# Spreading inverse roots by float32r products over twin rows in a two-block transformer kernel

## What is computed

```python
def first_block(x, mem, ...):
    for layer in range(DEPTH):
        h = rms_norm(x, mix_norm_g[layer])
        proj = h @ w_in[layer]
        da_q, da_k, da_v, sb_q, sb_k, sb_v, c_q, c_kv, k_r = jnp.split(proj, pts, axis=-1)
        y_a = diff_attention(da_q, da_k, ...)      # q and k normed per head of 64
        y_b = stick_breaking(sb_q, sb_k, sb_v, ...)
        y_c = latent_attention(c_q, c_kv, k_r, ...) # q and k normed per head of 96: 64 plain, 32 rotary
        y = jnp.concatenate([y_a, y_b, y_c], axis=-1)
        x = x + y @ w_out[layer]
        ...
```

## Time and profile before

| | us |
|---|---|
| median of 3 runs | 2628.76 (2628.24 to 2629.06) |
| profiled execution | 2626.96 |
| span in that execution, first to last instruction | 2625.2 |
| TensorE busy | 2572.9, 98% |
| GpSimd busy | 1313.6, 50% |
| VectorE busy | 1142.8, 44% |
| ScalarE busy | 677.7, 26% |
| mean granted clock of TensorE | 0.998 |

### The profile page before, as it was taken

One profiled execution on the slowest core, in us unless ns is written; L12 is line 12 of the kernel. 1 busy time (PEld: TensorE's weight loads), 2 busy tenths in 40 slices (PEclk: granted clock), 3 DMA queues, 4 the chain that ended last, 5 costly groups with the idle time before them and its releaser, 6 DMA issues.

```text
span 2625.2 us, 35579 instructions
## 1 busy us (share of the span) xinstructions
PE 2572.9 (98%) x14733; PEld 2058.6 (78%) x14733; DVE 1142.8 (44%) x1977; ACT 677.7 (26%) x1329; POOL 1313.6 (50%) x548
## 2 busy tenths in 40 slices
PE   7999999999999999999999999999999999999998
PEld 6877668888888776688888866888888877888887
DVE  4344464666543445546665345322224135322224
ACT  4236451111122454511111244200001333200002
POOL 5443136665565432255555732566555521566653
PEclk9999999999999999999999999999999999999999
DMA  7321124555332110335663211322222211222221
GB/s 246 95 59 33 33 90 135 193 189 185 120 100 81 59 48 29 102 118 188 191 192 113 84 49 33 107 96 96 96 96 96 81 49 33 81 96 96 96 96 64
DMA packets 222509, 265.38 MB, mean 101 GB/s; under 512 B 19248, under 2 KB 197000, under 8 KB 222248
## 3 DMA queue, kind: packets, MB, share of 16 engines
q1 hardware_dynamic: 219648, 256.58, 30.7%
q10 hardware_dynamic: 2728, 6.90, 0.8%
HBM read 258.74 MB, written 4.72 MB: 100 GB/s over the span
## 4 chain that ended last, share of the span: by engine, by line
PE 69%; ACT 1%; DVE 1%; POOL 0%; issue 0%; PEldq 0%; PEld 0%; DVEq 0%; ACTq 0%
PE PS L961 8%; PE PS L964 8%; PE PS L965 8%; PE PS L923 4%; PE PS L927 4%; PE PS L928 4%; PE PS L1672 2%; PE PS L1676 2%; PE PS L1675 2%; PE PS L1958 1%; PE PS L2011 1%; PE PS L1832 1%; PE PS L1799 1%; PE PS L942 1%; PE PS L945 1%; PE PS L948 1%
## 5 line engine op out<-in xcount | busy, mean ns | idle before, releaser
L833 POOL TENSOR_SCALAR WH<-RAW 128x2048 fp32r<-128x2048 f32 x178 | 342.2, 1923 | 1099.1 <-issue 906.5
L835 POOL TENSOR_TENSOR WL<-RAW,WH 128x2048 fp32r<-128x2048 f32 x178 | 822.5, 4621 | 14.8
L961 PE MATMUL PS<-Hh,WL 128*128 128x512 f32 x1152 | 448.6, 389 | 0.0
L964 PE MATMUL PS<-Hl,WH 128*128 128x512 f32 x1152 | 448.2, 389 | 0.0
L965 PE MATMUL PS<-Hh,WH 128*128 128x512 f32 x1152 | 448.1, 389 | 0.0
L2625 DVE SCALAR_TENSOR_TENSOR X<-PS,X 128x512 f32<-128x512 f32 x304 | 208.8, 689 | 189.4 <-PE PS L1676 127.6
L961 PEld LDWEIGHTS PS<-Hh,WL 128*128 128x128 f32 x1152 | 216.3, 188 | 45.3 <-issue 0.4
L965 PEld LDWEIGHTS PS<-Hh,WH 128*128 128x128 f32 x1152 | 216.3, 188 | 45.0
L964 PEld LDWEIGHTS PS<-Hl,WH 128*128 128x128 f32 x1152 | 216.3, 188 | 44.5
L3005 DVE TENSOR_TENSOR PS<-SQ,PS 128x512 f32<-128x512 f32 x44 | 30.6, 696 | 427.6 <-PE PS L965 427.6
L1672 PE MATMUL PS<-U,WL 128*128 128x512 f32 x512 | 202.3, 395 | 0.0
(11 more groups left out here) (550 smaller groups left out, 4703.9 us busy)
## 6 DMA issues: line engine op xcount, KB each, us to landing
RAW<-in_w_ff SPq DMA_DIRECT2D x64, 1024.0 KB, 5.5
PROJ<-in_ada_w SPq DMA_DIRECT2D x48, 1024.0 KB, 8.2
RAW<-in_ffn_w_in SPq DMA_DIRECT2D x44, 1024.0 KB, 5.1
RAW<-in_ffn_w_out SPq DMA_DIRECT2D x22, 1024.0 KB, 4.8
RAW<-in_w_in SPq DMA_DIRECT2D x20, 1024.0 KB, 5.5
RAW<-in_w_out SPq DMA_DIRECT2D x8, 1024.0 KB, 5.0
RAW<-in_a_w_in SPq DMA_DIRECT2D x6, 1024.0 KB, 5.1
RAW<-in_b_w_in SPq DMA_DIRECT2D x12, 512.0 KB, 4.6
```

Of the source, the lines that this page charges most:

```text
L833: pool.tensor_scalar(WH[b][:, :], RAW[b][:, :], 1.0, 1.0, ALU.mult, ALU.mult).then_inc(s.split_hi, 1)
L835: pool.tensor_tensor(WL[b][:, :], RAW[b][:, :], WH[b][:, :].bitcast(F32), ALU.subtract).then_inc(s.split_done, 1)
L961: ins = mm(bank, WL[b][:, col:col + P], Hh[:, k, :], start=k == 0, stop=False)
L964: mm(bank, WH[b][:, col:col + P], Hl[:, k, :], start=False, stop=False)
```

## The change

The spreads are made by single float32r products over tiles that hold twin rows. In each group of 32 rows, rows 0 to 15 hold the high half and rows 16 to 31 the rest of the same values; a spread matrix with ones in both rows adds them in one product.

- The column patterns that sum squares get their ones twice, 16 columns apart, so sums, roots and inverses come out in both rows.
- Head norms: VectorE's subtract (2663) becomes one scalar_tensor_tensor, which takes off the high half in the second of the twin rows only. `head_spread` makes four products instead of eight.
- Latents: ScalarE leaves the root in PS. VectorE inverts it there, copies it to float32r (`roots_hi`), and fills the twins by four scalar_tensor_tensor of 32 rows by 128 columns into a tile of 128x512 that it has set to zero at the start of the stage. TensorE makes six products over 512 columns (`latents_spread`) in the place of six calls of `token_spread`.
- The spread matrices grow from 2 to 6, so their transfer (line 715) from 128 to 384 KB and VectorE's turn to float32r from 256 to 768 columns.
- Two masks leave the constants and come by a transfer of their own (128 KB, 256 columns), issued ahead of the memory's; a third, unused one is dropped. VectorE waits for it with its first copy.
- A semaphore is saved in the memory attention, where `me.r` becomes a count of `me.m`.
- The list of the output steps and all else stays in its order.

```diff
@@ position_constants
-    c[0:HD, C_HALF] = 1
-    c[HD:P, C_HALF + 1] = 1
+    for twin in (0, TWIN):
+        c[0:HD, C_HALF + twin] = 1
+        c[HD:P, C_HALF + twin + 1] = 1
...
-    spread = np.zeros((P, 2, P), np.float32)
-    for b in range(2):
-        spread[2 * b:P:32, b, 0:HD] = 1
-        spread[2 * b + 1:P:32, b, HD:P] = 1
+    spread = np.zeros((P, SPREADS, P), np.float32)
+    for b in range(4):
+        spread[2 * b:P:TWIN, b, 0:HD] = 1
+        spread[2 * b + 1:P:TWIN, b, HD:P] = 1
+    for x in range(2):
+        for h in range(MLA_HEADS):
+            spread[4 * x + h:P:TWIN, 4 + x, MLA_ROPE * h:MLA_ROPE * h + MLA_ROPE] = 1
@@ transfers
+            sp.dma_start(masks_in, t["dist"][:, D_ALL:D_ALL + 2 * P]).then_inc(s.hot_in, 16)
...
-            sp.dma_start(PTS[:, 1, 0:256].rearrange("p (b c) -> p b c", b=2), t["spread"]).then_inc(s.lam_in, 16)
+            sp.dma_start(spread_in.rearrange("p (b c) -> p b c", b=SPREADS), t["spread"]).then_inc(s.lam_in, 16)
@@ head_spread
-                    mm(PS[:, banks[g], 0:n], spread[32 * g:32 * g + 32, q, :], inv_h[32 * g:32 * g + 32, 0:n], start=True, stop=False)
-                for g in range(4):
-                    n = width(4 * q + g)
-                    mm(PS[:, banks[g], 0:n], spread[32 * g:32 * g + 32, q, :], inv_l[32 * g:32 * g + 32, 0:n],
-                       start=False, stop=True).then_inc(a.bc, 1)
+                    mm(PS[:, banks[g], 0:n], spread[32 * g:32 * g + 32, q, :], inv_twins[32 * g:32 * g + 32, 0:n],
+                       start=True, stop=True).then_inc(a.bc, 1)
@@ TensorE, second stage
+                def latents_spread(bank, kind):
+
+                    mm(bank, spread[:, kind, :], twins, start=True, stop=True).then_inc(s.f_tile, 1)
+
...
                 for x in range(4):
-                    token_spread(feed(11 + x), TN_ML, 2 * x)
+                    latents_spread(feed(11 + x), x)
                 for x in range(2):
-                    token_spread(feed(15 + x), TN_ML, 4 * x, MLA_ROPE)
+                    latents_spread(feed(15 + x), 4 + x)
@@ ScalarE
-                    f(roots(n), PS[:, bank, 0:P], ACT.Sqrt, scale=scale, bias=bias).then_inc(mix.rt, 1)
+                    f(PS[:, bank, 0:P] if n == TN_ML else roots(n), PS[:, bank, 0:P], ACT.Sqrt, scale=scale, bias=bias).then_inc(mix.rt, 1)
@@ VectorE
-                v.tensor_tensor(inv_l, PS[:, 7, :], inv_h.bitcast(F32), ALU.subtract).then_inc(s.hri, 1)
+                v.scalar_tensor_tensor(inv_twins, inv_h.bitcast(F32), twin, PS[:, 7, :], ALU.mult, ALU.add).then_inc(s.hri, 1)
...
-            v.wait_ge(s.hot_in, 32)
+            v.wait_ge(s.hot_in, 48)
...
-            v.tensor_copy(spread[:, :, :], PTS[:, 1, 0:256].rearrange("p (b c) -> p b c", b=2))
+            v.tensor_copy(spread[:, :, :], spread_in.rearrange("p (b c) -> p b c", b=SPREADS))
...
+                def latents_inverse():
+
+                    root = PS[:, 5, 0:P]
+                    v.wait_ge(mix.rt, tn + TN_ML + 1)
+                    v.reciprocal(root, root).then_inc(mix.r_ml, 1)
+                    v.wait_ge(mix.r_ml, 2 * L + 1)
+                    v.tensor_copy(roots_hi, root).then_inc(mix.r_ml, 1)
+                    v.wait_ge(mix.r_ml, 2 * L + 2)
+                    for c in range(QT):
+                        r = slice(32 * c, 32 * c + 32)
+                        ins = v.scalar_tensor_tensor(twins[r, P * c:P * c + P], roots_hi[r, :].bitcast(F32), twin[r, :], root[r, :],
+                                                     ALU.mult, ALU.add)
+                    ins.then_inc(mix.r, 1)
+
+                v.memset(twins.bitcast(F32), 0.0)
...
-                token_inverse(TN_ML)
+                latents_inverse()
```

More of the change, by code:

```diff
@@ L89 @@
 SLOTS = 3
-C_ID, C_ONE, C_NTRI, C_NONE, C_SBM, C_SBN, C_RECT = [P * i for i in range(7)]
-C_EPS = C_RECT + P
+C_ID, C_ONE, C_NTRI, C_NONE = [P * i for i in range(4)]
+C_EPS = C_NONE + P
 C_SLA = C_EPS + 1
@@ L103 @@
 C_SEL = C_MX + 32
-C_ALL = C_SEL + 12 + 32
+C_TWIN = C_SEL + 12 + 32
+C_ALL = C_TWIN + 1
+TWIN = 16
+SPREADS = 6
 DIL_KEYS = S + 2 * P
@@ L131, in position_constants @@
     c[:, C_NONE:C_NONE + P] = -1
-    c[:, C_SBM:C_SBM + P] = p < f
-    c[:, C_SBN:C_SBN + P] = np.where(p < f, 0, NEG)
-    c[:, C_RECT:C_RECT + P] = np.where(f // CHUNK > p // CHUNK, NEG, 0)
     half = MLA_ROPE // 2
@@ L144, in position_constants @@
         c[:, C_SLB + o] = HD ** -0.5 / dil_slope(2 * o + np.arange(P) // HD)
-    c[0:HD, C_HALF] = 1
-    c[HD:P, C_HALF + 1] = 1
+    for twin in (0, TWIN):
+        c[0:HD, C_HALF + twin] = 1
+        c[HD:P, C_HALF + twin + 1] = 1
     c[:, C_WHOLE:C_WHOLE + 2] = 0.5
     for h in range(MLA_HEADS):
-        c[MLA_ROPE * h:MLA_ROPE * h + MLA_ROPE, C_QUART + h] = 1
-    c[:, C_CQ:C_CQ + MLA_HEADS] = MLA_DIM * EPS / 256
+        c[MLA_ROPE * h:MLA_ROPE * h + MLA_ROPE, [C_QUART + h, C_QUART + TWIN + h]] = 1
+    for twin in (0, TWIN):
+        c[:, C_CQ + twin:C_CQ + twin + MLA_HEADS] = MLA_DIM * EPS / 256
     c[:, C_MX:C_MX + MEM_HEADS] = HD * EPS / D
     c[:, C_SEL + 12] = 1
-    c[:, C_MLB] = np.where(np.arange(P) % 32 < MLA_HEADS, EPS * EPS, EPS)
+    c[:, C_MLB] = np.where(np.arange(P) % TWIN < MLA_HEADS, EPS * EPS, EPS)
+    c[:, C_TWIN] = -(np.arange(P) % 32 >= TWIN).astype(np.float32)
     c[:, C_YCB] = np.where(np.arange(P) % 32 < 2, 0, EPS)
-    spread = np.zeros((P, 2, P), np.float32)
-    for b in range(2):
-        spread[2 * b:P:32, b, 0:HD] = 1
-        spread[2 * b + 1:P:32, b, HD:P] = 1
+    spread = np.zeros((P, SPREADS, P), np.float32)
[5 more added lines that the diff above has]
+            spread[4 * x + h:P:TWIN, 4 + x, MLA_ROPE * h:MLA_ROPE * h + MLA_ROPE] = 1
     freqs = (np.float32(10000.0) ** (-np.arange(half, dtype=np.float32) / np.float32(half))).astype(np.float32)
@@ L177, in position_constants @@
     far = 1e30
-    d = np.zeros((P, D_ALL), np.float32)
+    d = np.zeros((P, D_ALL + 2 * P), np.float32)
+    d[:, D_ALL:D_ALL + P] = np.where(p < f, 0, NEG)
+    d[:, D_ALL + P:] = np.where(f // CHUNK > p // CHUNK, NEG, 0)
     u = np.arange(3 * P)[None, :]
@@ L288, in __init__ @@
         self.r = sem("mx_r")
+        self.r_ml = sem("mx_r_ml")
         self.yn = sem("mx_yn")
@@ L343, in __init__ @@
         self.tr = sem("me_tr")
-        self.r = sem("me_r")
         self.s = sem("me_s")
@@ L419, in build @@
         PROJR = nc.alloc_sbuf_tensor_at("PROJR", [P, 18, S], F32R, offset=proj_at)
-        spread = sb("spread_r", [P, 2, P], F32R)
+        spread = sb("spread_r", [P, SPREADS, P], F32R)
         arena_at = nc.sbuf_base
         ARENA = sb("ARENA", [P, 8 * S])
+        ARENAR = nc.alloc_sbuf_tensor_at("ARENAR", [P, 8 * S], F32R, offset=arena_at)
         U = nc.alloc_sbuf_tensor_at("U", [P, 2, 2, 2, S], F32R, offset=arena_at)
@@ L473, in build @@
         ntri, nones = C[:, C_NTRI:C_NTRI + P], C[:, C_NONE:C_NONE + P]
-        sbmask, sbneg, rect = C[:, C_SBM:C_SBM + P], C[:, C_SBN:C_SBN + P], C[:, C_RECT:C_RECT + P]
         ident_r, sbneg_r, rect_r = EXACT[:, 0, :], EXACT[:, 1, :], EXACT[:, 2, :]
+        rect = rect_r.bitcast(F32)
+        masks_in = ARENA[:, 2048:2048 + 2 * P]
         eps = C[:, C_EPS:C_EPS + 1]
         cos, sin = PROJ[:, 16, :], PROJ[:, 17, :]
-        inv_h, inv_l = INV[:, 0, :], INV[:, 1, :]
+        inv_h, inv_twins = INV[:, 0, :], INV[:, 1, :]
         sums_lhs = lambda x, whole: C[:, (C_WHOLE if whole else C_HALF) - 2 * x:(C_WHOLE if whole else C_HALF) - 2 * x + 32]
@@ L482, in build @@
         k_nope = ARENA[:, 0:1024].rearrange("p (t n) -> p t n", t=2)
-        roots = lambda n: ARENA[:, 1024 + P * (n % 2):1024 + P * (n % 2) + P]
+        roots = lambda n: ARENA[:, 1792 + P * (n % 2):1792 + P * (n % 2) + P]
+        twins = ARENAR[:, 1024:1536]
+        roots_hi = ARENAR[:, 1920:1920 + P]
+        twin = C[:, C_TWIN:C_TWIN + 1]
         eps_l = ARENA[:, 1536:1792].rearrange("p (t i c) -> p t i c", t=2, i=QT)
@@ L547, in da_dense @@
             return [x // 8 if x < 64 else 4 + x // 16 for x in da_steps(u) if (x % 8 == 7 if x < 64 else x % 16 == 15)]
+        spread_in = PTS[:, :, :].rearrange("p a n -> p (a n)")[:, 256:256 + SPREADS * P]
         squares = SQ[:, 0, :], SQ[:, 1, :], PTS[:, 0, :], PTS[:, 1, :]
@@ L2675, in _ @@
             v.wait_ge(s.const_in, 16)
-            v.wait_ge(s.hot_in, 32)
+            v.wait_ge(s.hot_in, 48)
             v.tensor_copy(RS[0:32, 0, 0:P].rearrange("p (m c) -> p m c", m=8),
                           projf[0:32, 6144 + REL:6144 + REL + 8].rearrange("p (m o) -> p m o", o=1).to_broadcast([32, 8, 16])).then_inc(s.su_rb, 1)
-            for x, y in enumerate((ident, sbneg, rect)):
+            for x, y in enumerate((ident, masks_in[:, 0:P], masks_in[:, P:2 * P])):
                 v.tensor_copy(EXACT[:, x, :], y)
@@ L2907, in _ @@
                 v.wait_ge(me.tr, L + 1)
-                v.reciprocal(mem_rs, PS[:, 3, 0:P].rearrange("p (i x) -> p i x", i=QT)[:, :, 0:MEM_HEADS]).then_inc(me.r, 1)
```

(5 more changed lines are left out.)

## The result

| | before, us | after, us |
|---|---|---|
| median of 5 runs | 2628.24 (2626.65 to 2629.06) | 2639.77 (2638.26 to 2641.82) |
| profiled execution | 2626.96 | 2638.26 |
| its span | 2625.2 | 2636.5 |
| mean granted clock | 0.998 | 0.995 |

The changed kernel takes 1.0044 times as long (95% interval 1.0030 to 1.0058), 11.5 us more. The prediction was 2636.0 with a range to 2639.5: the direction and the mechanism hold, the median lies 0.3 above the range. The profiled execution is 11.3 us longer than that of before, where the sum said 7.3.

A forecast was written before the change was run, and what follows sets the result against it. TensorE, busy 98% of the span, was taken to bound the kernel. The terms -1.3 - 3.4 + 8.7 + 3.0 + 0.3 gave +7.3 us, so 2636.0 us from a median of 2628.76, with a range of 2624 to 2639.5.

The forecast's parts named there:

- Head norms: TensorE's queue in four head norm calls: dropping the second group of products saves 0.33 us each, -1.3 us in all.
- Latents' spreads: TensorE ahead of the fifth output step: six products paced by VectorE's takings save 1.7 us a layer, -3.4 us.
- Inverse and additions: Longer latents' inverse delays the rope additions behind GpSimd; TensorE stalls 4.35 us a layer before the third output step, +8.7 us.
- Clock: Behind each new TensorE stall the granted clock falls once, at 1.5 us: +3.0 us, bounds 0 and 3.4.
- Setup: Setup stage: the spreads' wider cast on VectorE delays GpSimd's split and the first stage, +0.3 us.
- A: The forecast itself: TensorE stalls in both layers, 2633 to 2639 us; chance 0.63.
- B: No stall: VectorE keeps its turn for the second rope addition, or the inverse ends before 228.6; 2624.4 us; chance 0.19.
- C: Stall before the third output step in one layer only, or half as long: 2628.8 to 2630.3 us; chance 0.10.
- D: The spreads aren't shortened because VectorE's takings don't close up: +3.4 us on any case; chance 0.03.
- E: More is gained than VectorE seems to allow: below 2623 us; chance 0.05.

The follow-up runs named there:

- the extra reciprocal: Kernel before plus one scratch reciprocal behind the latents' reciprocal, 128 columns in one run, 64 in another: ratios 1.0041 and 1.0044, medians 2641.92 and 2641.39 us.
- the additions first: Changed kernel with the latents' inverse moved between the two rope additions and the first output residual: ratio 1.0017 to the kernel before, median 2634.69 us.
- the inverse later: Changed kernel with the latents' inverse moved behind the first softplus: ratios 0.9979 and 0.9989 to the kernel before, medians 2624.86 and 2623.80 us.
- the 8.1 us wait: Changed kernel, latents' inverse behind the first softplus, plus two unread products behind each spread, which made TensorE wait for bank 5: ratio 1.0055 to the kernel before.
- the longer reciprocal: Kernel before plus one scratch reciprocal of 128 columns (0.86 us) behind the latents' reciprocal: ratio 1.0041, median 2641.92 us.
- the two that were filled: Changed kernel with 22 unread products on TensorE in each layer's gap ahead of the third output step: ratio 1.0031 to the kernel before, median 2639.11 us.

## Why the prediction was wrong by its size and right by its mechanism

**Head norms**, -1.3. The rows say 0.23 a call (0.67 to 0.44), -0.9. I took the distance between the two groups of the earlier trace rows as the price of one, but a group that stands alone holds TensorE for 0.44 and not for 0.33; why isn't shown. The distances above (156.92 less 156.47 for two calls) agree.

**Latents' spreads**, -3.4. Between 31.89 and 33.55 lie 1.66 a layer: -3.3. VectorE's takings do set it, at 0.66 a step.

**Inverse and additions**, +8.7. The inverse took 2.77, not 2.37: the waits for itself cost the 0.04 assumed, but the four quarters start 0.36 apart, not 0.27. That changed nothing, as the sum said (a later arrival ends at the same place). Second addition 5.03, residual at 236.33 (forecast 236.05, in a timeline that is 0.24 later by then), gap 4.2 a layer by the waits, 4.4 by the step's start (4.61 later less the 0.23 by which the kernel was late there): 8.7 to 8.8. Confirmed, and by the extra reciprocal shown without the change.

**Clock**, +3.0: the step that failed. The term of the sum was one fall per stall at 1.5 us, with 3.4 as the bound for both stalls, taken from a wait of 2.04. Seven of eight gaps of 4.1 to 4.2 us (two profiles of the change, two kernels with an extra reciprocal, two layers each) brought 6.8 us at half rate, the eighth (layer 1 of after) 3.3. By the distances the seven cost 2.4 to 3.0 us each, not 1.5: of the 6.8 us, 0.7 to 1.8 lie in the gap itself, and half of the rest is lost. In the first profile of the change it was 2.95 in layer 0 (the offset to before grows from 4.61 at the step's start to 7.56 at line 1389) and 1.72 in layer 1, together 4.7; in the second 2.6 and 2.6, together 5.2. Both lie above the bound of 3.4. In the profiled pair two more falls came in (near 370, +1.5, and behind layer 1's spreads, +1.7) and that near 1080 went (-1.7): 6.2 in all. The row that I took was half as long as the gap, and I used it as if a fall had one size. The evidence for the lower bound was an accident too: the wait of 2.30 that "left it at 1.00" did so in one execution; in the other twelve profiles a wait of 2.2 to 2.6 stands there and the clock fell behind it, near 35.

**Setup**, +0.3. GpSimd's split behind the cast, which waits for it, takes 4.76 or 4.77 in all nine profiles with the new setup and 4.57 or 4.58 in the four with the old one:

```profile
28.78 4.76 POOL L850 TENSOR_TENSOR WL<-RAW,WH 128x2048 fp32r<-128x2048 f32 x1
```

The first stage starts 1.0 behind its end in both kernels (33.89 and 34.54), so the cost is 0.19. In the profiled pair the first stage starts 0.65 later; the other 0.46 is that the split begins later, behind the transposes of x, which took a median of 421 ns each against 273. That varies from execution to execution: the first addition of the bias mask lies at 69.18 to 69.89 in four profiles with the old setup and at 68.89 to 72.60 in nine with the new one.

The sum with measured terms: -0.9 - 3.3 + 8.7 + 6.2 + 0.65 = +11.35, beside 11.3 between the profiled spans. That fit owes something to the choice of falls of two executions. With the clock at its usual price behind the gaps (2 x 2.65, an estimate from the seven), no other falls and 0.2 for the setup the sum is +10.0. The medians say 11.5 on the first chip and 10.0 on another. The two kernels with an extra reciprocal, which lack the gains of 4.2, should stand some 4 above the change and were at +11.3 and +12.3; their intervals are 3.4 us wide to either side, so the times don't settle it. The distances do for the larger part: 40.3 to 40.6 a layer, against 38.9 in the second profile of the change.

**The rivals.** A came, with two falls of more than the assumed size; its own range ended at 2639. B (VectorE keeps its turn) is refuted by eight additions of 5.03 or 5.04 in four executions (two profiles of the change, two kernels with the extra reciprocal). C needed one layer without a stall: none. D and E didn't come. What I left out is A with longer falls, 0.9 to 1.5 more for each gap by the price of the seven, and that is what came most often. That the median lay only 0.3 above the range is no merit of the term.

**Open.** Why the clock falls near 35, 205, 370, 925 and 1090 in one execution and not in the next isn't known. Each of these places lies behind waits of TensorE that every profile has: 2.2 to 2.6 us near 35 (a fall in twelve of thirteen profiles), 2.04 us near 370 and 1090 (nine of twenty-six), three of 0.58 to 0.77 us near 205 and 925 (ten of twenty-six). The falls behind the spreads (255 and 975 with the additions first, 970 with the inverse later, 980 in after) came in four of the twelve layers in which TensorE makes six spreads in a row with pauses of 0.15 to 0.56 (those with the 8.1 us wait not counted), and in none of the ten with the 64 narrow products. Whether the pauses cause them isn't shown, since the experiment for that made another wait.

## What to carry to other kernels

Before VectorE gets a longer instruction, look up what GpSimd starts in the time after it, and which of VectorE's next instructions read two SBUF operands: the arrival decides, by 0.4 us here, whether one of them waits for a GpSimd instruction of 4.6 us. Work that nobody needs soon belongs behind such a pair, not ahead of it; the same instructions made the kernel 0.4% slower at one place and 0.1 to 0.2% faster at the other. A new gap of TensorE is priced as its length plus what follows at half rate, and for a gap of 4 us that was 2.4 to 3.0 us on top in seven cases of eight. A range for such a term needs more than one profile of the same kernel: one execution is one choice of falls.

## What the runs showed of the hardware

- An addition with two SBUF inputs, 512 columns, issued 0.18 us behind the start of GpSimd's split, was held until its end: 2.28 instead of 0.81. The one behind it was held for the next GpSimd instruction, although VectorE came to it right behind the first: 5.03. The Trainium skill's page "SBUF — State Buffer", section "Who interferes with whom", states that a VectorE instruction with two SBUF inputs contends with a GpSimd instruction that reads SBUF, and that the order of issue decides who is held; the trace agrees. The prediction called it turn-taking. In every case here the instruction that went next was also the one that had been asked for first (GpSimd's at 230.80, the second addition some 0.4 later), so no run tells turns from the order of asking. With the additions early the first one waited too, for GpSimd's second rope multiply (1.67, in both layers of the later inverse), without harm.
- The half-rate time came in pieces of about 3.4 or 6.8 us, once 10.3, and the piece didn't follow from the length of the gap alone: 3.4 behind gaps of 2.4 (both layers), 6.8 behind 4.1 to 4.2 (seven of eight, 3.3 in the eighth), 6.8 and 10.3 behind 8.1, but also 6.9 behind a wait of 2.04 (near 1100 in the kernel with the longer reciprocal). All twelve gaps of 2.4 us and more that the experiments made brought a fall; the two that were filled to 0.44 and 0.48 brought none.
- The clock could fall while TensorE stood still: at about 236.3 in after, 0.7 us before the next product.
- The setup's 32 transposes of x took 421 ns each at first and 272 later, in stretches with a granted clock of 1.00 throughout; what makes the difference isn't known.
